# Expert weight ring of 12 slots instead of 11, with the 64-place activations in another part of SBUF

## The reference, cut to what matters

```python
def moe_swiglu(h, w_router, w_gu, w_down):
    def fn(t):
        logits = (t @ w_router).astype(jnp.float32)
        top_v, top_i = lax.top_k(logits, TOP_K)
        top_w = jax.nn.softmax(top_v, axis=-1)
        gate = jnp.sum(jax.nn.one_hot(top_i, N_EXPERTS, dtype=jnp.float32) * top_w[..., None], axis=1)
        gu = jnp.einsum('nd,edf->nef', t, w_gu)
        act = jax.nn.silu(gu[..., :FFN_EXPERT]) * gu[..., FFN_EXPERT:] * gate[..., None].astype(t.dtype)
        return jnp.einsum('nef,efd->nd', act, w_down)
```

## Time and profile before

| | |
|---|---|
| median of 3 runs | 1399.47 us (1395.12, 1399.47, 1400.95) |
| the profiled execution | 1399.31 us |
| its span in the trace | 1397.6 us |
| TensorE matmul busy | 1348.5 us (96%) |
| VectorE, ScalarE busy | 793.0 us (57%), 673.6 us (48%) |
| DMA | 431.69 MB, mean 309 GB/s |

### The profile page before, as it was taken

How to read it: one execution, slowest core, us unless ns; L and a number is a source line. 1 busy time by engine, 2 the same in 40 slices (tenths; PEclk the granted TensorE clock), 3 DMA queues, 4 the chain that set the end, 5 groups by cost and what they waited for, 6 DMA issues and landing times.

```text
span 1397.6 us, 19214 instructions
## 1 busy us (share of the span) xinstructions
PE 1348.5 (96%) x7452; PEld 992.3 (71%) x7452; DVE 793.0 (57%) x880; ACT 673.6 (48%) x834; POOL 39.3 (3%) x96
## 2 busy tenths in 40 slices
PE   7999999998999998999999999999999999999896
PEld 7987888887985476777676766676666667666662
DVE  6855655545857858874376643367644266744332
ACT  5556544435557856763365632356542256623221
POOL 7000000001000000000000000000000000000000
PEclk9999999999999999999999999999999999999999
DMA  8453555554543035999999989999999999999997
GB/s 346 155 178 106 199 194 186 181 189 151 193 170 121 1 117 228 336 373 422 421 421 422 420 324 422 420 421 421 421 371 422 420 421 421 422 367 422 421 421 289
DMA packets 59993, 431.69 MB, mean 309 GB/s; under 512 B 6656, under 2 KB 6656, under 8 KB 7808
## 3 DMA queue, kind: packets, MB, share of 16 engines
q1 hardware_dynamic: 59760, 429.95, 77.5%
q10 hardware_dynamic: 144, 0.52, 0.1%
HBM read 429.40 MB, written 1.05 MB: 308 GB/s over the span
## 4 chain that ended last, share of the span: by engine, by line
PE 83%; DMA 11%; DVE 3%; ACT 2%; issue 0%; POOL 0%; SPq 0%; POOLq 0%; DVEq 0%; ACTq 0%
PE bank L1529 20%; PE bank L1531 19%; PE bank L1530 19%; DMA raw<-in_moe 11%; PE bank L2029 7%; PE bank L2050 6%; PE bank L1877 2%; PE bank L1903 2%; DVE w_lo L1434 1%; PE bank L1887 1%; PE bank L1976 1%; ACT w_hi L841 1%; PE bank L2077 1%; PE bank L1905 1%; DMA raw<-in_wts 1%; PE bank L1984 1%
## 5 line engine op out<-in xcount | busy, mean ns | idle before, releaser
L1434 DVE TENSOR_TENSOR w_lo<-raw,w_hi 128x2048 fp32r<-128x2048 f32 x130 | 295.8, 2288 | 237.0 <-ACT w_hi L841 236.7
L841 ACT ACTIVATE w_hi<-raw 128x2048 fp32r<-128x2048 f32 x130 | 248.0, 1916 | 257.2 <-DMA raw<-in_moe 229.5
L1529 PE MATMUL bank<-w_hi,ht_hi 128*128 128x512 f32 (+1 forms) x768 | 302.7, 394 | 0.9 <-DVE ht_lo L975 0.9
L1531 PE MATMUL bank<-w_hi,ht_lo 128*128 128x512 f32 (+1 forms) x768 | 296.6, 386 | 0.0
L1530 PE MATMUL bank<-w_lo,ht_hi 128*128 128x512 f32 (+1 forms) x664 | 255.3, 385 | 0.0
L943 DVE TENSOR_TENSOR w_lo<-raw,w_hi 128x2048 fp32r<-128x2048 f32 x73 | 166.6, 2289 | 109.9 <-ACT w_hi L517 109.7
L517 ACT ACTIVATE w_hi<-raw 128x2048 fp32r<-128x2048 f32 x74 | 141.4, 1918 | 95.7 <-PE bank L1531 92.9
L1529 PEld LDWEIGHTS bank<-w_hi,ht_hi 128*128 128x128 f32 x768 | 144.3, 188 | 44.8 <-issue 14.8
L1531 PEld LDWEIGHTS bank<-w_hi,ht_lo 128*128 128x128 f32 x768 | 144.3, 188 | 30.0
L2029 PE MATMUL bank<-raw,xb 128*64 128x256 f32 x1280 | 147.1, 381 | 0.0
L1530 PEld LDWEIGHTS bank<-w_lo,ht_hi 128*128 128x128 f32 x664 | 125.0, 188 | 23.3
(11 more groups left out here) (336 smaller groups left out, 1586.9 us busy)
## 6 DMA issues: line engine op xcount, KB each, us to landing
raw<-in_moe SPq DMA_DIRECT2D x247, 1024.0 KB, 15.2
more<-in_moe SPq DMA_DIRECT2D x89, 1024.0 KB, 15.7
raw<-in_wts SPq DMA_DIRECT2D x71, 1024.0 KB, 4.8
xs<-in_x SPq DMA_DIRECT2D x2, 512.0 KB, 3.9
out<-xn SPq DMA_DIRECT2D x4, 256.0 KB, 2.0
pk<-in_packed SPq DMA_DIRECT2D x1, 517.0 KB, 8.2
g1b<-in_norm_ffn ACTq DMA_DIRECT2D x1, 512.0 KB, 3.6
gfb<-in_norm_final SPq DMA_DIRECT2D x1, 512.0 KB, 20.1
```

The lines of the kernel that those rows point to most:

```text
L841: a(w_hi[:, hi_order(n) % SPLIT, :], slot_raw(n), ACT.Copy).then_inc(s_hi, 1)
L1434: v.tensor_tensor(slot_lo(n), slot_raw(n), w_hi[:, hi_order(n) % SPLIT, :].bitcast(F32), ALU.subtract).then_inc(s_lo, 1)
L1529: mm(out_, sh, mh, start=first, stop=False)
L1531: return mm(out_, sl, mh, start=False, stop=last)
```

## The change

The ring gets a twelfth buffer, `more3`, which lies over `pk`, `ws_hi` and `ws_lo`. Its first slot is number 82, which waits for slot 71 to be used. `sgb` and `avb` move to the idle half of `ht_lo`. Nothing else is edited; RING is now 12, so -84 mod 12 is 0.

```diff
-RAW, EXTRA, SPLIT = 8, 3, 4
+RAW, EXTRA, SPLIT = 8, 4, 4
 RING = RAW + EXTRA
...
-    ident, _ = sb("ident", [P, P])
+    ident, ident_at = sb("ident", [P, P])
...
-    more_at = (hk_at, hk_at + KD * T * 4, a0 + 22 * T * 4 + 28 * P * 4)
+    more_at = (hk_at, hk_at + KD * T * 4, a0 + 22 * T * 4 + 28 * P * 4, pk_at)
+    assert pk_at + SLOT * 4 <= ident_at
...
-    sgb, _ = sb("sgb", [P, 2, 256], F32, pk_at)
-    avb, _ = sb("avb", [P, 2, 256], F32, pk_at + 2 * 256 * 4)
+    sgb, _ = sb("sgb", [P, 2, 256], F32, ht_at + KD * T * 4 + 4 * T * 4)
+    avb, _ = sb("avb", [P, 2, 256], F32, ht_at + KD * T * 4 + 6 * T * 4)
...
-    TURNS = [n % RAW for n in range(N0 - RAW, N0 - 4)] + [RAW, RAW + 1] + [n % RAW for n in range(N0 - 4, N0)] + [RAW + 2]
-    EXTRA_FREE = (VV0 + 2, VV0 + 2, N0)
+    TURNS = [n % RAW for n in range(N0 - RAW, N0 - 4)] + [RAW, RAW + 1] + [n % RAW for n in range(N0 - 4, N0)] + [RAW + 2, RAW + 3]
+    EXTRA_FREE = (VV0 + 2, VV0 + 2, N0, N0 + 1)
```

## The result

The changed kernel took 1380.85 us, the median of four runs (1379.56 to 1382.96), against 1398.09 for the kernel before. The ratio is 0.9878, with a 95% interval of 0.9852 to 0.9905. The forecast was 1383.0, faster by over 0.5%, with 1379 to 1388 as its main case.

A forecast was written before the change was run, and what follows sets the result against it. The prediction took TensorE and the weight loads as almost balanced, with loads stalled at ring jumps. Loads would gain 16.5 + 2.5 = 19.0 us, but TensorE's waits capped this: 1399.31 - 16.5 = 1382.8, so 1383.0 as median; main case 1379 to 1388.

The forecast's parts named there:

- The bound: Experts' part: TensorE and loads nearly balanced, loads losing 2.2 us a round; issue stalls of 12.3 us at round starts.
- The jump: Loads after slots 183, 267 and 351 no longer wait for the slot seven back; loads regain 16.5 us.
- The slot of lead: Every load from 83 on is released one use earlier, putting the loads 2.5 us ahead for good.
- TensorE then becomes the other end: End of the experts' part: TensorE gains at most its 16.5 us of waits, so the last use comes at 1370.1.
- The sign that went with this step: From 840 us on, TensorE's waits for split weights fall from 14.9 to under 2 us.
- The queue's margin: End of first heavy half: issue-to-landing time falls to 7.5 us, 2.7 above a lone load's 4.8; priced at zero.
- rival A: Queue thins to single loads at heavy halves' ends, giving back 7 us or more; about 1390; chance 0.14.
- Rival B: Loads have only the one-slot head start to regain; 2.5 us won, 1397; chance 0.08.
- Rival C: Instruction fetches find no gap among unbroken loads on their queue; slower by 7 us; chance 0.03.
- The moved tiles: `sgb` and `avb`, written 28 times each at another address: bounded by 0.6 us either way, taken as 0.
- The clock piece: Clock at 0.91 in 1320 to 1340 costs 1.8 us; may go with the waits, kept for the low end.

The follow-up runs named there:

- E1: Changed kernel, but the first seven loads of rounds 2, 3 and the last wait for the slot seven back, as with 11 slots; 1397.09 us, ratio 1.0005.
- E2: Changed kernel with 12 buffers, but every load from 83 on waits for the slot eleven back, without a jump; 1383.7 us, ratio 0.9901.
- E3: Changed kernel with the waits for the slot seven back only at the first jump (loads 183 to 189); 1389.14 us, ratio 0.995.
- E7: Changed kernel with the waits for the slot seven back only at the two later jumps (loads 267 to 273, 351 to 357); 1390.09 us, ratio 0.9961.
- E9: Changed kernel, but loads 83 to 110, issued in the first stage, wait for the slot eight back, later ones twelve; 1389.56 us, ratio 0.9955.
- E8: Changed kernel without the second of three matmuls in the 14 split down slots of the last light half, loads unchanged; 1380.11 us, ratio 0.9883.
- E6: Changed kernel, but every load from 83 on waits for the slot eight back, without a jump; 1395.25 us, ratio 0.999.
- E4: Kernel before with its ring of 11, only `sgb` and `avb` moved to the idle half of the low gathered tokens; 1396.44 us, ratio 0.9994.
- E5: The changed kernel as it is, timed again as comparison for the second series; 1379.53 us, ratio 0.9878.

## Why the prediction was right

**The bound, right.** The prediction read an almost even balance of TensorE and the loads from the stages, and the loss from SP's issues at slots 183, 267 and 351. E1 puts back only those waits and gets back the whole time of before. One reading was off: the loads were to lose 2.2 us a round to TensorE. Rounds 2 and 3 of TensorE take 208.2 us even without a wait, 2 x 104.6 us is 209.2, and so they lose only 1.0. The prediction had worked with the first round, which is 1.9 us shorter (206.35 us from 619.73 to 826.08 after the change).

**The jump, 16.5 us, right in kind, a little too large.** The change without the twelfth slot's depth (E2) gives 13.4 us. The landings in the trace say much the same: of the loads 182 to 190, 266 to 274 and 350 to 358 of the kernel before, the last landed some 7.7, 2.6 and 3.9 us later than a load every 2.485 us (1.0486 MB at 422 GB/s) would have it, some 14 us together; in the changed kernel all three are 0.0. What else the six windows of 20 us lacked was not taken apart. Nor do the shares stand on their own: E3 and E7 cost 9.6 and 10.6.

**The slot of lead, 2.5 us, right within what the runs can tell.** It measured 2.6 between the traces of E2 and the changed kernel, and 4.2 between the medians. Four slots of it, taken away in the first stage alone, cost 10.0 us (E9).

**"TensorE then becomes the other end", wrong.** The step had the loads done in time for a last use at 1367.7 and let TensorE's 16.5 us of waits set 1370.1. The last use came at 1370.16, but by the loads, which landed last at 1368.16, where 1365.7 was forecast. Two errors met. The loads' path was too early: the jumps had cost them some 14 us, not 16.5. And TensorE's path was too late: 4.2 us of its waiting stood in its busy time, so it had more to give than the waits' rows show. E8 shows which of the two sets the end. That the number came out within 3 us is in part luck: the sum was capped by a row that happened to lie near what the loads could really gain, 16.0. Without the cap the two terms for the loads, 16.5 and 2.5, give 19.0, 3 us too much. The sign that went with this step failed as well: the waits for split weights were to fall under 2 us and fell to 4.1.

**The queue's margin, right for 12 slots.** The prediction had the time to landing fall to 7.5 us near 827; it stayed at 9.3 in 800 to 825 and the queue did not run dry. But the margin was counted from the wrong place, 4.8 us, where a load is alone. E6 shows rival A real at a depth of eight, with 7.2 us from issue to landing: at the 7.5 us of the forecast there would have been little margin left. Rival B fell by E1 and E2. Rival C, slower instruction fetch, has nothing for it: TensorE shows no new idle time.

**The moved tiles, right** (E4). **The clock piece, left in the time, but worth nearly nothing:** the stretch at 0.91 came again in 1320 to 1340, beside the waits that are left. In E5, the same program, it didn't come:

```profile
1320.00:1340.00 20.00, 18.36 (x114) 11.94 (x114) 6.42 (x5) 5.74 (x6) 0.00 (x0) 1.00 1.02 422
```

E5's experts' part takes 828.9 us against 829.4. So the 1.8 us that the prediction held ready for the low end are at most 0.5 by this pair, which is to be expected where the loads set the end.

## What to carry to other kernels

Where a ring's walk must start each round of a loop at the same place, the jump that this takes shortens the ring for a whole pass. A size that divides the round has none, and here that was worth 13 us or more where the extra slot by itself was worth some 3. Look at the issue times at the seams of the rounds, not at the mean depth: the loss shows in TensorE only later, here some 50 us (load 183 was issued at 811.96, and the first matmul that had to wait starts at 863.91). And when two engines are this close to balance, test by taking work off one of them before saying which one sets the end, since "busy" rows hold waiting too.

## What was not expected of the hardware

Part of the scatter between executions is the granted clock ahead of the experts. Window 400 to 420, first the profiled execution of the changed kernel, then that of E5, which is the same program:

```profile
400.00:420.00 20.00, 17.87 (x108) 14.08 (x107) 8.85 (x15) 8.51 (x23) 0.00 (x0) 0.74 0.19 62
```

```profile
400.00:420.00 20.00, 17.87 (x143) 14.93 (x141) 12.63 (x22) 10.02 (x27) 0.00 (x0) 1.00 0.29 106
```

TensorE stands idle for 2.13 us ahead of the same matmuls in both (busy 17.87 of 20). In one the clock falls to its lower level (1.2 GHz) behind that and in the other it stays at 2.4. From the first matmul behind the wait (404.20 and 405.47) to the first expert slot's use (540.77 and 537.88) it is 136.6 us in the one and 132.4 in the other: the fall costs 4.2 us. Their spans are 1381.1 and 1377.8 us. E2's profile has the 0.74 too, and its first expert slot comes at 542.5. The other nine profiles, with that of the kernel before, have 1.00 there. The clock is not all of the scatter: the kernel before uses its first expert slot at 541.2 all the same, having come to this wait only at 408.75. What decides whether the clock falls was not tried. By the Trainium skill (TensorE: Matmul & The Clock Gate, HAM oscillation), waits of TensorE are what lets the gate throttle it; the trace agrees in that the fall follows a wait, and shows that the same wait need not bring it.
